# A norm's mean square on all partitions, root and reciprocal on whole rows, and a new order of the early loads

## The reference, cut to what matters

```python
def _rmsnorm(x, gain):
    xf = x.astype(jnp.float32)
    y = xf * lax.rsqrt(jnp.mean(xf * xf, axis=-1, keepdims=True) + NORM_EPS)
    return (y * gain.astype(jnp.float32)).astype(x.dtype)

def _modulate(x, gain, shift, scale):
    return _rmsnorm(x, gain) * (1 + scale) + shift

# layer i: six chunks (shift, scale, gate, twice) of 1024 values
mod_lat = jnp.split((jax.nn.silu(c) @ ada_w[i] + ada_b[i])[:, None, :], MOD_CHUNKS, axis=-1)
h_lat = _modulate(x_lat, norm1_g[i], mod_lat[0], mod_lat[1])
x_lat = x_lat + mod_lat[2] * mixer(h_lat)
f_lat_in = _modulate(x_lat, norm2_g[i], mod_lat[3], mod_lat[4])
x_lat = x_lat + mod_lat[5] * _peer(f_lat_in, ...)
# at the end: _rmsnorm(x_lat, final_gain)

# mixer of layer 0
z = _gelu(h @ w_in);  u, v = z[..., :2048], z[..., 2048:]
sv = einsum('gpq,bnqgd->bnpgd', w_s, _rmsnorm(v, v_gain)) + b_s
y = (u * sv) @ w_out
```

## Time and profile before

| | |
|---|---|
| median of 3 runs | 1863.58 us (1859.71 to 1865.44) |
| the profiled execution | 1865.96 us, of it the span 1864.2 us |
| PE busy | 1840.4 us (99%) |
| DVE, ACT, POOL busy | 1508.8, 962.6, 447.7 us |
| granted TensorE clock, mean over the span | 0.998 |
| DMA | 376.33 MB, mean 202 GB/s |
| chain that ended last | PE 90%, DVE 4%, DMA 3% |

### The profile page before, as it was taken

The page is one execution under the profiler, slowest core; times in us unless marked ns, Lnnn a source line. Parts: engine busy times, 40 slices in busy tenths (PEclk is TensorE's granted clock), DMA queues, the critical chain, the costliest instruction groups (busy, mean ns, idle before and its releaser), DMA issues.

```text
span 1864.2 us, 35462 instructions
## 1 busy us (share of the span) xinstructions
PE 1840.4 (99%) x11760; PEld 1585.6 (85%) x11760; DVE 1508.8 (81%) x2800; ACT 962.6 (52%) x1608; POOL 447.7 (24%) x225
## 2 busy tenths in 40 slices
PE   8999999999999999999999999999999999999998
PEld 7899998888888888888888998888888888878887
DVE  7684789978998888888888588997999888886555
ACT  6554455655555444445555445565555544445554
POOL 6136578870000000000001258884000000000000
PEclk9999999999999999999999999999999999999999
DMA  8866455556645555588874445556555555555554
GB/s 340 315 240 225 159 179 183 189 187 210 214 169 174 176 170 179 169 293 319 319 285 159 147 160 190 182 189 204 203 203 172 173 174 174 175 169 192 191 192 134
DMA packets 104177, 376.33 MB, mean 202 GB/s; under 512 B 12464, under 2 KB 12464, under 8 KB 103856
## 3 DMA queue, kind: packets, MB, share of 16 engines
q1 hardware_dynamic: 103392, 373.37, 58.7%
q0 software_dynamic: 432, 2.10, 0.3%
q10 hardware_dynamic: 288, 0.06, 0.0%
HBM read 374.43 MB, written 1.05 MB: 201 GB/s over the span
## 4 chain that ended last, share of the span: by engine, by line
PE 90%; DVE 4%; DMA 3%; ACT 1%; POOL 1%; issue 1%; SPq 0%; ACTq 0%; DVEq 0%; POOLq 0%
PE ring L1778 22%; PE O L1833 13%; PE O L1835 12%; PE O L1834 12%; PE ring L1780 11%; PE ring L1750 3%; PE ring L1493 2%; PE ring L1495 2%; PE ring L1494 2%; PE ring L1771 2%; DMA raw<-in_u 1%; PE O L1771 1%; PE ring L1752 1%; DVE wL L901 1%; ACT wH L532 1%; PE O L1623 1%
## 5 line engine op out<-in xcount | busy, mean ns | idle before, releaser
L532 ACT ACTIVATE wH<-raw 128x1024 fp32r<-128x1024 f32 x597 | 634.3, 1062 | 818.1 <-DMA raw<-in_v 366.0
L1778 PE MATMUL ring<-hX,wH 128*128 128x512 f32 x1984 | 704.3, 399 | 0.1
L901 DVE TENSOR_TENSOR wL<-raw,wH 128x1024 fp32r<-128x1024 f32 x384 | 470.3, 1225 | 174.2 <-ACT wH L532 170.4
L1780 PE MATMUL ring<-hX,wL 128*128 128x256 f32 x1984 | 555.1, 280 | 0.0
L1778 PEld LDWEIGHTS ring<-hX,wH 128*128 128x128 f32 x1984 | 372.5, 188 | 86.9 <-issue 0.9
L1833 PE MATMUL O<-wH,gateH 128*128 128x512 f32 x1024 | 405.1, 396 | 0.0
L1835 PE MATMUL O<-wH,gateL 128*128 128x512 f32 x1024 | 399.5, 390 | 0.0
L1834 PE MATMUL O<-wL,gateH 128*128 128x512 f32 x1024 | 398.3, 389 | 0.0
L1780 PEld LDWEIGHTS ring<-hX,wL 128*128 128x128 f32 x1984 | 374.6, 189 | 0.0
L494 POOL TENSOR_TENSOR wL<-raw,wH 128x1024 fp32r<-128x1024 f32 x128 | 316.8, 2477 | 54.8 <-ACT wH L532 53.7
L1835 PEld LDWEIGHTS O<-wH,gateL 128*128 128x128 f32 x1024 | 192.2, 188 | 41.4
(11 more groups left out here) (213 smaller groups left out, 2419.6 us busy)
## 6 DMA issues: line engine op xcount, KB each, us to landing
raw<-in_u SPq DMA_DIRECT2D x256, 512.0 KB, 3.3
raw<-in_v SPq DMA_DIRECT2D x256, 512.0 KB, 3.3
ada_v<-in_ada SPq DMA_DIRECT2D x40, 512.0 KB, 4.4
raw<-in_w_q SPq DMA_DIRECT2D x30, 512.0 KB, 3.3
ada_m<-in_ada SPq DMA_DIRECT2D x24, 512.0 KB, 5.2
raw<-in_w_in SPq DMA_DIRECT2D x23, 512.0 KB, 4.5
ada_f<-in_ada SPq DMA_DIRECT2D x16, 512.0 KB, 15.1
raw<-in_w_out SPq DMA_DIRECT2D x16, 512.0 KB, 4.0
```

The lines of the kernel that those rows point to most:

```text
L532: nc.scalar.activation(wH[s % RAW][:, :], (place or raw[s % RAW])[:, :], ACT.Copy).then_inc(s_h, 1)
L901: nc.vector.tensor_tensor(wL[s % RAW][:, :], raw[s % RAW][:, :], wH[s % RAW][:, :].bitcast(fp32), ALU.subtract).then_inc(s_low, 1)
L1778: mm(bank[:, :], wH[s][:, k * P:k * P + P], hX[:, k, :, :].rearrange("p two t -> p (two t)"), start=(k == 0), stop=False)
L1780: ins = mm(bank[:, 0:T], wL[s][:, k * P:k * P + P], hH[:, k, :], start=False, stop=(k == KT - 1))
```

## The change

`mean` becomes one matmul for each j, with `mean_w` stationary and the 256 squares moving, into `O[0]`: every partition holds the mean of all tokens. ACT takes the root of 128x256 values from `O[0]` into `O[2]` (`O[1]` in norm 0), DVE takes the reciprocal of 128x256 values in place there, and waits for itself; `spread` and its semaphore go. `ada_m` has six buffers instead of four, each with its own semaphore, and all 24 loads go through `load_early`, which waits for `s_acc >= m - 5`. The order of the loads changes: number 16 to 19 and the six small loads come before the `w_v` tiles 12 to 15, number 20 and 21 behind them, 12 loads in `w_u`, six in `w_out`, the first of these behind tile 3; the two halves of `keys` are loaded behind the first four `w_q` tiles, and PE waits for them at the first scores. In norm 0 `low_h(0, 1)` comes ahead of six `rooted`. Between the layers ACT splits the third `p_in` tile after the squares, and DVE makes its first half inside norm 2, after k = 3. The last `front_raw` buffer is `ada_f[0]`.

```diff
@@ -152,13 +150,14 @@
-        for under, count in ((64, 4), (88, 2), (100, 3)):
+        for under, count in ((64, 4), (88, 2), (104, 2)):
...
+        front_raw.append(ada_f[0])
         with ExitStack() as ad:
-            sb("under_ada_m", [P, 112 * T], at=ad)
-            ada_m = [sb(f"ada_m{x}", [P, D], at=ad) for x in range(4)]
+            sb("under_ada_m", [P, 104 * T], at=ad)
+            ada_m = [sb(f"ada_m{x}", [P, D], at=ad) for x in range(6)]
...
+        def root_rows(n):
+            return O[2 if n else 1][:, 0:T]
...
+        U_LOADS = (0, 2, 3, 4, 5, 6, 8, 9, 10, 11, 12, 13)
+        U_ADA = (0, 1, 2, 4, 5, 6, 7, 8)
+        OUT_LOADS = (3, 5, 7, 9, 11, 12)
+
+        def gate_slot(m):
+
+            return (m - ADA_FRONT + 2) % 6
...
+            def load_early(m):
+
+                if m >= ADA_FRONT + 4:
+                    sp.wait_ge(s_acc, m - 6 + 1)
+                sp.dma_start(ada_m[gate_slot(m)][:, :], ada_d[m]).then_inc(s_gates[gate_slot(m)], 16)
...
@@ -384,26 +401,25 @@
-            m = ADA_FRONT
+            for m in range(ADA_FRONT, ADA_FRONT + 4):
+                load_early(m)
+            for dst, src in small_loads:
+                sp.dma_start(dst, src).then_inc(s_small, 16)
             for t in range(BLOCK_TILES, 16):
                 load_gate(t)
-                load_ada(ada_m, m, first=True)
+            m = ADA_FRONT + 4
+            for t in range(2):
+                load_early(m)
                 m += 1
-            load(stream_dram["w_u", 0], W_U, 0, 0)
-            for dst, src in small_loads:
-                sp.dma_start(dst, src).then_inc(s_small, 16)
             for t in range(16):
-                if t:
-                    load(stream_dram["w_u", 0], W_U, t // 4, t % 4)
-                if t < 8 or t > 11:
-                    load_ada(ada_m, m)
+                load(stream_dram["w_u", 0], W_U, t // 4, t % 4)
+                if t in U_LOADS:
+                    load_early(m)
                     m += 1
-            sp.dma_start(keys[:, 0], k1_d[0]).then_inc(s_keys, 16)
-            sp.dma_start(keys[:, 1], k2_d[0]).then_inc(s_keys, 16)
             for t in range(16):
                 load(stream_dram["w_out", 0], W_OUT, t // 4, t % 4)
-                if 4 < t < 13:
-                    load_ada(ada_m, m)
+                if t in OUT_LOADS:
+                    load_early(m)
                     m += 1
...
                     if layer == 0:
+                        sp.wait_ge(s_acc, ADA_U0)
+                        sp.dma_start(keys[:, 0], k1_d[0]).then_inc(s_keys, 16)
+                        sp.dma_start(keys[:, 1], k2_d[0]).then_inc(s_keys, 16)
...
             def root(n):
-                for tt in range(TT):
-                    act.wait_ge(s_ms, TT * n + tt + 1)
-                    nc.scalar.activation(std[:, tt:tt + 1], O[tt][:, 0:1], ACT.Sqrt, bias=eps[:, :]).then_inc(s_std, 1)
+                act.wait_ge(s_ms, n + 1)
+                nc.scalar.activation(root_rows(n), O[0][:, 0:T], ACT.Sqrt, bias=eps[:, :]).then_inc(s_std, 1)
...
-                if layer < LAYERS - 1:
-                    ahead(base, 31, 3)
                 for j in range(KT):
                     act.wait_ge(s_res, KT * layer + j + 1)
                     square(j)
+                if layer < LAYERS - 1:
+                    ahead(base, 31, 3)
                 norm(2 * layer + 2)
...
             def inverse_root(n):
-                dve.wait_ge(s_std, TT * (n + 1))
-                nc.vector.reciprocal(inv[:, :], std[:, :]).then_inc(s_inv, 1)
+                dve.wait_ge(s_std, n + 1)
+                nc.vector.reciprocal(root_rows(n), root_rows(n)).then_inc(s_inv, 1)
...
                 inverse_root(n)
-                dve.wait_ge(s_rstd, n + 1)
+                dve.wait_ge(s_inv, n + 1)
...
+                    if k == 3 and n == 2:
+                        low_first(BASE["p_in", 1], 0, 2)
...
                 if k == 0:
                     inverse_root(0)
-                elif k == 2:
+                else:
+                    low_h(0, k - 1)
+                if k == 2:
                     for j in range(2, KT):
                         last = rooted(j)
                     nc.vector.memset(tick[:, 0:1], 0.0).then_inc(s_rooted, 1)
-                    low_h(0, 1)
-                else:
-                    low_h(0, k - 1)
...
-                        if t < 8:
-                            ada_tile(ada_m, m)
+                        if t in U_ADA:
+                            ada_early(m)
                             m += 1
...
-                if layer == 0:
-                    low_first(base, 31, 6)
                 norm(2 * layer + 2)
...
                 pe.wait_ge(s_sq, KT * n + j + 1)
-                for tt in range(TT):
-                    ins = mm(O[tt][:, 0:P], sq[:, j, tt * P:tt * P + P], mean_w[:, :], start=(j == 0), stop=(j == KT - 1))
-                    if j == KT - 1:
-                        ins.then_inc(s_ms, 1)
-
-            def spread(n, bank=None):
-
-                pe.wait_ge(s_inv, n + 1)
-                for tt in range(TT):
-                    ins = mm((O[2] if bank is None else bank)[:, tt * P:tt * P + P], inv[:, tt:tt + 1].to_broadcast([P, P]), ident[:, :],
-                             start=True, stop=True)
-                ins.then_inc(s_rstd, 1)
+                ins = mm(O[0][:, 0:T], mean_w[:, :], sq[:, j, :], start=(j == 0), stop=(j == KT - 1))
+                if j == KT - 1:
+                    ins.then_inc(s_ms, 1)
...
             def scores(layer, j):
 
+                if layer == 0 and j == 0:
+                    pe.wait_ge(s_keys, 32)
```

More of the change, by code:

```diff
@@ L131, in build @@
         vstd = sb("vstd", [P, TT])
-        std = sb("std", [P, TT])
-        inv = sb("inv", [P, TT])
         cond = sb("cond", [P, D])
@@ L199, in build @@
         s_ada = [sem(f"s_ada{x}") for x in range(4)]
+        s_gates = [sem(f"s_gates{x}") for x in range(6)]
         s_front = [sem(f"s_front{x}") for x in range(16)]
@@ L224, in build @@
         s_inv = sem("s_inv")
-        s_rstd = sem("s_rstd")
         s_first_l = sem("s_first_l")
@@ L348, in load, with load_ada @@
                 sp.dma_start(raw[s % RAW][:, :], tile).then_inc(s_raw[s % RAW], 16)
-            def load_ada(place, m, first=False):
-                if not first:
-                    sp.wait_ge(s_acc, m - len(place) + 1)
+            def load_early(m):
+                if m >= ADA_FRONT + 4:
+                    sp.wait_ge(s_acc, m - 6 + 1)
+                sp.dma_start(ada_m[gate_slot(m)][:, :], ada_d[m]).then_inc(s_gates[gate_slot(m)], 16)
+            def load_ada(place, m):
+                sp.wait_ge(s_acc, m - len(place) + 1)
                 sp.dma_start(place[m % len(place)][:, :], ada_d[m]).then_inc(s_ada[m % 4], 16)
@@ L362, in load_gate @@
                 if t in FRONT_RAW:
+                    if t == FRONT_RAW[-1]:
+                        sp.wait_ge(s_acc, 1)
                     sp.dma_start(front_raw[t - 3][:, :], stream_dram["w_v", 0][t]).then_inc(s_fraw[t - 3], 16)
@@ L924, in ada_front, with ada_tile, ada_early @@
                 add_ada_psum(ada_f[n], n // 2 + (KT, 0)[n % 2])
-            def ada_tile(place, m, psum=False):
-                dve.wait_ge(s_ada[m % 4], 16 * ((m - ADA_FRONT) // 4 + 1))
-                (add_ada_psum if psum else add_ada)(place[m % len(place)], m)
+            def ada_tile(place, m):
+                dve.wait_ge(s_ada[m % 4], 16 * ((m - ADA_U0) // 4 + 1))
+                add_ada(place[m % len(place)], m)
+            def ada_early(m, psum=False):
+                dve.wait_ge(s_gates[gate_slot(m)], 16 * ((m - ADA_FRONT + 2) // 6 + (gate_slot(m) > 1)))
+                (add_ada_psum if psum else add_ada)(ada_m[gate_slot(m)], m)
             def modulations(lo_chunk, hi_chunk, norms, unit=None):
@@ L1027, in _ @@
                     dve.wait_ge(s_x, 16)
-                    dve.wait_ge(s_rstd, 1)
+                    dve.wait_ge(s_inv, 1)
                 if k < 2:
@@ L1102, in _ @@
                             for _ in range(OUT_ADA[2 * j + s]):
-                                ada_tile(ada_m, m, psum=True)
+                                ada_early(m, psum=True)
                                 m += 1
@@ L1638, in _ @@
             keep_clock(6)
-            spread(0, O[1])
             keep_clock(8, ring[2])
@@ L1722, in _ @@
                         mean(3, j - 2)
-                if layer == 0:
-                    pe.wait_ge(s_keys, 32)
                 n = 2 * layer + 1
@@ L1731, in _ @@
                 keep_clock(4, O[3])
-                spread(n)
                 keep_clock(5)
@@ L1873, in _ @@
                     keep_clock(4, O[3])
-                spread(2 * layer + 2)
                 if layer == 0:
```

## The result

| | before | after |
|---|---|---|
| median, timed side by side, 9 runs each | 1865.41 us (1859.71 to 1867.24) | 1875.27 us (1868.31 to 1875.96) |
| ratio, 95% interval | | 1.0055 (1.0045 to 1.0066) |
| profiled execution, of it the span | 1865.96, 1864.2 us | 1875.28, 1873.5 us |
| granted clock, mean over the span | 0.998 | 0.996 |

The change makes the kernel slower by about 10 us. Two repeats on other chips gave 1.0065 (1.0048 to 1.0082) and 1.0050 (1.0038 to 1.0062), 9 to 12 us. The forecast was 1864.4 us in a range of 1858.0 to 1870.0, so the time lies outside the range. Of the 10.9 us between 1864.4 and 1875.27, 1.8 are no part of the change: the kernel before itself had a median of 1865.41 here, against the 1863.58 that the forecast started from.

A forecast was written before the change was run, and what follows sets the result against it. PE, busy 99% of the span, was taken as the bound. Front 0, `w_u` -4.7, `w_out` +3.1 and norms 1 to 4 +2.45 sum to +0.85 us: 1863.58 + 0.85 = 1864.4 us, range 1858.0 to 1870.0.

The forecast's parts named there:

- `w_u`, -4.7: `w_u` stage: tile 1's late load and the clock fall behind it go, -5.4 us; 0.7 us back at tile 4.
- `w_out`, +3.1: `w_out` stage: SP's wait for ada tile 28 delays tile 4, PE idles 5.2 us, clock falls; +3.1 us, bounds +1.5 and +6.
- The reciprocal, 2.0 us: Norms: DVE's reciprocal of 256 columns takes 2.0 us (line 1.76, bounds 0.41 and 4.0); +0.95 us each in norms 1, 3, 4.
- Norm 2, -0.4: Norm 2, between the layers: root to `scaled` 2.5 instead of 3.21 us, -0.7; 0.3 back for DVE's half split at k = 4.
- GpSimd holds DVE back in norm 2: Rival, norm 2: the first `low_h` waits for GpSimd's halves until 992.5 instead of running near 990.7; +1.9 us, 1866.3; chance 0.12.
- Front, 0: Front (norm 0): earlier `low_h(0, 1)` and DVE's delay by the reciprocal cancel; 0 us, bounds -1.2 and +2.2.
- Mean, 0: Norms 1 to 4: the mean has as many moving columns as before, so it costs 0 us.
- Experts, 0: Expert stages of both layers, from 190 to 970 us and again in layer 1: not touched, 0 us.
- The harmless wait: Rival, `w_out`: DVE takes ada tile 28 some 4 us sooner, so the stage gains 3.0 us; 1858.3 us, chance 0.17.
- the cheap reciprocal: Rival, norms: the reciprocal takes 0.41 us, so four norms gain 1.6 us each; 1858.0 us, chance 0.08.
- the late loads: Rival, `w_u`: tile 1 still comes late because ada tiles share the DMA, no 4.7 us gain; 1869.1 us, chance 0.08.
- The clock in the norms: Rival, norms 1, 3 and front: PE's longer idling lowers the clock, three falls of 1.7 us each; 1869.5 us, chance 0.15.

The follow-up runs named there:

- e2: Kernel after with ACT's split of the third `p_in` tile ahead of the squares again, DVE's half still inside norm 2: 1870.21 us, 1.0030.
- e5: Kernel before with the new form of the norm alone; loads, seam and front order as before: 1872.43 us, 1.0038.
- e3: Kernel after with the norm of the kernel before (single columns, `spread`), new loads and new seam kept: 1870.64 us, 1.0024.
- e4: Kernel after with the old norm, `w_out` ada loads behind tiles 5, 7, 9, 10, 11, 12, and ACT's split ahead of the squares: 1858.30 us, 0.9966.
- e8: Kernel after with old norm, later `w_out` ada loads, ACT's split ahead of the squares, and DVE's half ahead of norm 2: 1859.92 us, 0.9968.
- r3: Kernel before, unchanged, run again for a third trace: both expert stages together 1596.6 us.
- e1: Kernel after with the six `w_out` ada loads behind tiles 5, 7, 9, 10, 11, 12 instead of 3, 5, 7, 9, 11, 12: 1866.51 us, 1.0018.

## Why the prediction was wrong, step by step

- **`w_u`, -4.7: right.** -6.1 in the first pair, -5.1 on average. ACT's idling ahead of the split of tile 1 is 1.82 us (at 64.44) instead of the 5.31 of the earlier trace rows, PE doesn't wait, and there is no clock fall. The 0.7 us that I had put back for tile 4 did not come.
- **`w_out`, +3.1: the mechanism was right, the sizes were off.** The wait at tile 4 came where it was put, at 5.9 us where 5.2 were forecast; the landing took 4.65 us where 4.5 were taken. Tile 4 began 137.72 - 120.15 = 17.6 us after the first `w_out` matmul, against 141.1 - 124.6 = 16.5 in the sum; 0.9 of the difference is SP's issue, 129.44 - 120.15 = 9.3 us against 133.0 - 124.6 = 8.4, since DVE took ada tile 28 that much later after PE's last `w_u` tile. The other error is the clock: I had taken over 1.7 us from a stretch of 3.4 us behind a wait of 3.71 us, and here it was 6.8 us, with 2.8 lost. That was the step "I add the same 1.7 us". With 1.1 and 1.1 more the term becomes 5.3, near the 5.4 measured. Over all nine traces with this wait (5.7 to 6.0 us) the loss was 2.0 us on average, so that 1.7 was low, but by less than the first pair says. In the means (+6.0) another 1.3 us come from before: this stage took 53.7, 51.0 and 52.6 us there, and the old waits of 3.0 us that the sum took away were 1.5 and 2.0 us in the repeats.
- **The reciprocal, 2.0 us: right, and the line through the rows was better than my choice.** The line gave 1.76 and the instruction takes 1.766 us; root to `scaled` is 2.28 in norms 1 to 4, so each of norms 1, 3 and 4 costs +0.7 to 0.8 there, not +0.95. The repeat count of 8 in the Trainium skill (VectorE: DVE Perf Modes, section First, the fixed hardware budget), read as 8 cycles for a column, would have made it 2.13 us, an estimate from that page; the measured slope is 6.3 ns for a column, so here the rows decide.
- **Norm 2, -0.4: wrong, by 2.6 us, and the chance of the rival was misjudged.** The rival "GpSimd holds DVE back in norm 2" had 0.12 and is what happened. The step that failed was the inference from the front, "beside 24.3 us of GpSimd's work in the front most `low_h` were not held". Those that were not held hardly met it there. Taken one by one, the `low_h` of 0.47 us in the front of the kernel before began while no half ran or in the last 0.11 us of one:

```profile
30.97 0.47 DVE L955 SCALAR_TENSOR_TENSOR hX<-sq,mod,hX 128x256 fp32r<-128x256 f32 x1
```
```profile
29.70 1.37 POOL L488 TENSOR_TENSOR wL<-front_raw,wH 128x512 fp32r<-128x512 f32 x1
```

The two that began with more of a half ahead, 1.06 us at 22.84 and 0.52 us at 45.81, took 1.34 and 0.80 us, and in all nineteen traces no `low_h` of the front took 0.47 us that began more than 0.11 us before the end of a half. In norm 2 it began 1.06 us before the end of the second half. The nearer row was 11, the same place and the same three halves: there DVE's instruction had already waited until all three were through. The rule of the Trainium skill (SBUF — State Buffer, section Terms: the shared port pair is exclusive and held for the full instruction, and the loser blocks) spoke for it, and the trace agrees, with 2.57 us beside GpSimd's halves; e2 shows 0.48 us as soon as the two don't meet. The rival's price of 1.9 us (1.8 by its own times, 992.5 and 990.7) was nearly right for the hold (995.3 against some 993.2, 2.1 us) and lacked the clock fall behind it, 1.7 us.
- **Front, 0: wrong, +1.0 to +1.7.** `low_h(0, 1)` came at 21.33, sooner even than I had counted, and PE's wait of 2.6 us on it is gone, with the 3.4 us at half clock that followed it at 25.5 in the kernel before. It gained nothing, because what PE needs next comes from ACT and GpSimd: 2.6 and 2.0 us of waits on L566 and L507 in its place. Counted from the root of norm 0 the parts can be told: `w_u` begins 53.3 us behind it in all three traces of before, 54.8 in e5 (old order, new norm), 53.8 to 55.4 in e3, e4 and e8 (new order, old norm), and 54.7 to 56.6 in the eleven with both. So the reciprocal costs 1.5 us in the old order, nearly whole, and the new order by itself costs 0.4 to 2.0 us here instead of gaining up to 1.2; with it the reciprocal adds about 1.0 on average. I had let two terms cancel, of which one had the wrong sign; what in the new order costs this was not tested. The upper bound of +2.2 held for the first pair and for the means.
- **Mean, 0: nearly right.** The matmuls take as long as before, but one root waits for a matmul of 256 columns where the first root waited for one of 128: 1.25 us from the last square to the root in norm 3 instead of 1.07, and 1.12 instead of 1.01 in norm 4. In norm 1 ACT waits 1.09 us for it instead of 0.58, since the last mean here stands behind fillers that PE had begun 0.9 us later.
- **Experts, 0: too sure, and in part wrong.** The first pair has 4.1 us here. Over nineteen traces the new addresses go with 2.1 us, of which the 0.7 of the query tiles are shown and the rest is open. I had let "untouched" stand for "the same", and a scatter of 1596.1 to 1603.0 us had no place in my range.
- **The other rivals.** The harmless wait fell with PE's 5.9 us, the cheap reciprocal with 1.766 us, the late loads with the `w_u` stage. The clock in the norms: no fall in norms 1 and 3, in any trace: PE's idling there is 1.5 us. The falls came in `w_out` and norm 2, behind longer waits.

Together: experts +4.1, norm 2 +2.6, `w_out` +2.3, front +1.0, `p_in` and `p_out` +0.3, and `w_u` -1.4 with the other norms -0.45, make 8.45, the difference between the +9.3 of the pair and the forecast of +0.85. All misses but two went to one side. The range had the bounds of `w_out` and of the front in it, but not both together with the rival of norm 2.

## What to carry to other kernels

Before a whole-row form replaces a per-token one, price the reciprocal by its columns: here what matmuls and handovers saved was less than the 1.6 us that 254 more columns of it cost. Where a load with a wait moves up in a queue, look at what stands behind it; the remedy is one place in a list, and it turned this order from a loss into a gain. When a step moves on one engine, ask which of its followers on GpSimd will now meet DVE's reads on the critical path, and give the clock behind a longer PE wait bounds of its own: the wait of 3.7 us had cost 1.7 us, those of 5.7 to 6.0 us cost 1.4 to 2.9.

## What the runs showed of the hardware that I had not expected

- The reciprocal of VectorE costs 165, 253 and 1766 ns for 2, 16 and 256 float32 columns, 6.3 ns for a column all along the line, where an addition over the same 256 columns takes 432 ns.
- A `SCALAR_TENSOR_TENSOR` of 0.47 us was held through two GpSimd instructions without a gap (2.57 us, kernel after) and through three (3.39 us, e3), and did not get in between them, where at 45.81 in the front one of 0.80 us did get in after the first. One that begins in the last 0.1 us of a GpSimd instruction can go either way: at 30.97 in the kernel before it took 0.47 us, at 30.57 in the kernel after 1.60 us, held through the next.
- TensorE's clock fell to 1.2 GHz for 3.4 us after PE had idled for 3.2 and 3.7 us in `w_u`, 2.6 us in the front, and 2.4 and 2.2 us in e5 (`w_u`, `w_out`); it did not fall after 2.6 us in `w_u` of r3 and 2.2 us in the front of e4. Around the end of 5.7 to 6.0 us of idling in `w_out` it was at 1.2 GHz for 6.8 us, from 1.0 to 4.0 us before PE went on. In norm 2 the same waits were followed by 3.4 us at half clock in most traces, by 6.8 in one of the kernel after, and by none in e1: what PE idled does not settle it alone.
- Sixteen bytes in the addresses of buffers moved the median of 512-column matmuls from 392 to 396 ns, in ten traces of ten, and back in three of three. `hX` and `wH`, which these matmuls read, lie ahead of the dropped buffers and did not move; which of the moved ones does it stays open.
